# Feed-forward lower products taken one unit at a time instead of the first two as a pair

## The reference

```python
D_FF = 2816
def conv_ffn(h, w_up, w_dw, b_dw, w_down):
    u = dwconv(h @ w_up, w_dw, b_dw)          # 3 taps along the tokens
    a, b = jnp.split(u, 2, axis=-1)
    return (jax.nn.silu(a) * b) @ w_down
...
    h_lat = h_lat + g2 * conv_ffn(b_lat, ffn_w_up[i], ffn_w_dw[i], ffn_b_dw[i], ffn_w_down[i])
    if not last:
        h_ctx = h_ctx + cg2 * conv_ffn(b_ctx, ffn_w_up[i], ffn_w_dw[i], ffn_b_dw[i], ffn_w_down[i])
```

## Time and profile before

| | us |
|---|---|
| median of 3 runs | 2795.96 (2792.84 to 2804.22) |
| profiled execution, its own time | 2798.08 |
| its span | 2796.2 |
| PE busy | 2484.9 (89%) |
| DVE busy | 1188.6 (43%) |
| ACT busy | 856.3 (31%) |
| mean granted TensorE clock | 0.938 of full |

### The profile page before, as it was taken

How to read it: one execution, slowest core, us unless ns; L and a number is a source line. 1 busy time by engine, 2 the same in 40 slices (tenths; PEclk the granted TensorE clock), 3 DMA queues, 4 the chain that set the end, 5 groups by cost and what they waited for, 6 DMA issues and landing times. The chain is left out here.

```text
span 2796.2 us, 35301 instructions
## 1 busy us (share of the span) xinstructions
PE 2484.9 (89%) x14376; PEld 1771.3 (63%) x14376; DVE 1188.6 (43%) x1741; ACT 856.3 (31%) x1305; POOL 29.7 (1%) x57
## 2 busy tenths in 40 slices
PE   5988798999999989899899998888897879999986
PEld 3872477888888776577687876665677653333322
DVE  2688235552355232474563552454333252222323
ACT  4210335331233142384542332455334240100001
POOL 0000000000000001100000000000000000000000
PEclk7998698999999989899899998899899979999998
DMA  5138311121112125101232232210232429999996
GB/s 219 56 98 298 126 47 52 60 75 54 53 60 72 57 99 201 65 2 58 69 102 80 91 106 66 72 54 3 74 99 68 158 85 409 412 410 410 412 415 242
DMA packets 93557, 390.88 MB, mean 140 GB/s; under 512 B 9072, under 2 KB 33904, under 8 KB 65264
## 3 DMA queue, kind: packets, MB, share of 16 engines
q1 hardware_dynamic: 93424, 388.97, 37.4%
HBM read 380.22 MB, written 2.10 MB: 137 GB/s over the span
## 5 line engine op out<-in xcount | busy, mean ns | idle before, releaser
L259 DVE TENSOR_TENSOR WLO<-RAW,WHI 128x1024 fp32r<-128x1024 f32 (+3 forms) x226 | 279.1, 1235 | 807.6 <-ACT WHI L248 807.6
L275 PE MATMUL PS<-XNH,WHI 128*128 128x512 f32 (+1 forms) x1856 | 580.4, 358 | 34.2 <-DVE WLO L259 14.5
L275 PE MATMUL PS<-XNL,WHI 128*128 128x512 f32 (+1 forms) x1856 | 579.9, 357 | 0.0
L275 PE MATMUL PS<-XNH,WLO 128*128 128x512 f32 (+1 forms) x1856 | 575.9, 355 | 0.0
L248 ACT ACTIVATE WHI<-RAW 128x1024 fp32r<-128x1024 f32 (+3 forms) x226 | 241.0, 1068 | 985.4 <-PE PS L275 896.9
L275 PEld LDWEIGHTS PS<-XNH,WHI 128*128 128x128 f32 x1856 | 314.8, 190 | 94.5 <-DVE WLO L259 24.7
L275 PEld LDWEIGHTS PS<-XNH,WLO 128*128 128x128 f32 x1856 | 317.2, 190 | 53.2
L275 PEld LDWEIGHTS PS<-XNL,WHI 128*128 128x128 f32 x1856 | 316.3, 190 | 50.1 <-issue 0.9
L2334 PE MATMUL PS<-RAWM,XS 128*64 128x512 f32 x912 | 216.3, 602 | 19.9 <-DMA RAWM<-experts 19.1
L2334 PEld LDWEIGHTS PS<-RAWM,XS 128*64 128x64 f32 x912 | 59.0, 136 | 144.1 <-issue 77.8
L582 DVE SCALAR_TENSOR_TENSOR C<-V,PRM,C (+1 forms) x120 | 126.0, 1050 | 11.8 <-DVE C L582 9.4
(11 more groups left out here) (309 smaller groups left out, 2975.6 us busy)
## 6 DMA issues: line engine op xcount, KB each, us to landing
RAWM<-experts SPq DMA_DIRECT2D x171, 1024.0 KB, 15.9
ADAW<-ada SPq DMA_DIRECT2D x48, 1024.0 KB, 8.5
RAW<-up SPq DMA_DIRECT2D x88, 512.0 KB, 3.3
RAW<-down SPq DMA_DIRECT2D x32, 704.0 KB, 4.1
X<-experts SPq DMA_DIRECT2D x21, 1024.0 KB, 18.3
RAW<-pw SPq DMA_DIRECT2D x24, 512.0 KB, 3.4
V<-V SPq DMA_DIRECT2D x64, 101.0 KB, 2.6
RAW<-qkv SPq DMA_DIRECT2D x12, 512.0 KB, 3.3
```

Source lines behind the costliest of these rows:

```text
L259: dve.tensor_tensor(prog.WLO[:, at % SPLITS, 0:to.length], prog.RAW[:, at % RAWS, 0:to.length], f32(prog.WHI[:, at % SPLITS, 0:to.length]) ...
L275: last = pe.matmul(prog.PS[:, to, a:b], w, x[:, k, a:b], start=(k == 0 and n == 0), stop=(k == g.k - 1 and n == 2))
```

## The change

A new function `multiply_behind` takes the lower units one at a time, all through `multiply`. Only unit 0 has the waits for the hidden chunks, through the new argument `ready`; the wait for unit 1's weights now stands at the start of unit 1. `conv_ffn` calls it for the lower products of both groups. The number of matmuls is the same.

```diff
--- before.py
+++ after.py
@@ -260,7 +260,7 @@
                       f32(prog.WHI[:, at % SPLITS, 0:to.length]), ALU.subtract).then_inc(prog.weights_lo, 1)
 
 
-def multiply(prog, pe, g, i, s, xh, xl, segments, psum_free, before=0):
+def multiply(prog, pe, g, i, s, xh, xl, segments, psum_free, before=0, ready=None):
 
     slot = (g.base + s) % SPLITS
     pe.wait_ge(prog.weights_lo, g.base + 4 * i + s + 1)
@@ -268,6 +268,8 @@
     to = (before + s) % 4
     last = None
     for k in range(g.k):
+        if ready is not None:
+            ready(k)
         wh = prog.WHI[:, slot, k * P:(k + 1) * P]
         wl = prog.WLO[:, slot, k * P:(k + 1) * P]
         for n, (w, x) in enumerate(((wh, xh), (wh, xl), (wl, xh))):
@@ -296,6 +298,16 @@
                 step(i, s)
     for u in range(4 * max(rounds, 1), g.n):
         step(u // 4, u % 4)
+
+
+def multiply_behind(prog, pe, g, xh, xl, segments, psum_free, ready, before):
+
+
+    multiply(prog, pe, g, 0, 0, xh, xl, segments, psum_free, before, ready)
+    for s in range(1, 4):
+        multiply(prog, pe, g, 0, s, xh, xl, segments, psum_free, before)
+    for u in range(4, g.n):
+        multiply(prog, pe, g, u // 4, u % 4, xh, xl, segments, psum_free, before)
 
 
 def multiply_first(prog, pe, g, xh, xl, segments, psum_free, ready, wait=lambda i, s: None, before=0):
@@ -1007,8 +1019,8 @@
             for grp in range(2):
                 multiply_all(prog, pe, ups[grp], prog.XNH, prog.XNL, lambda u: segments, psum_free,
                              None if grp else chunks_of(pe, norm), before=first(grp, False))
-                multiply_all(prog, pe, downs[grp], HH, HL, lambda u: segments, psum_free,
-                             lambda k: pe.wait_ge(hid_lo[grp], 2 + k + 1), before=first(grp, True))
+                multiply_behind(prog, pe, downs[grp], HH, HL, segments, psum_free,
+                                lambda k: pe.wait_ge(hid_lo[grp], 2 + k + 1), first(grp, True))
 
 
 def collect(prog, g, segments_of, dest_of, loads=(), before=None, load_after=None):
```

## The result

The changed kernel took 2754.41 us (median of 4 runs, 2750.2 to 2769.6) against 2797.26 us; the ratio is 0.9867 with a 95% interval of 0.9841 to 0.9892. Two later comparisons of the same kernel gave 0.9862 (0.9842 to 0.9881) and 0.9898 (0.9879 to 0.9918). All 15 timed executions of it average 2759.4 us, and the 37 of the kernel before in the same and the later comparisons 2794.5: 35.1 us less, where 31.3 was forecast. The three later comparisons ran on different chips, so ratios and differences within one comparison are the safer figures.

A forecast was written before the change was run, and what follows sets the result against it. PE, busy 89% of the span, was taken as the bound, so its idle and half clock cost time. Removing 31.98 us at four places, less 0.7 of new waits, took 2795.96 to 2765 us, range 2757 to 2775.

The forecast's parts named there:

- The gaps: Lower feed-forward units, two places per layer: PE's idle before units 0 and 2 goes, with half clock behind; 31.98 us.
- The wait for chunk 10: Lower unit 0: PE waits 0.34 us for this chunk at each layer 1 place, none in layer 0; costs 0.7 us.
- The dips stay: Rival at the four places: half-clock stretches do not hang on these gaps, only idle goes; 2772.7 us, chance 0.09.
- Chunk 10 binds: Rival in layer 1: both places wait for this chunk and a clock dip follows each; 2767.9 us, chance 0.09.
- Hidden anyway: Rival: a later stage gives the gain back, most likely where DMA is the bound; 2796 us, chance 0.04.
- Slower: Rival in layer 0's second group: unbroken work lowers the clock to 1.2 GHz; 2858 us, chance 0.02.
- The sum: Whole kernel: 31.98 us gained less 0.7 lost gives 31.3 us less, so 2765 us against the median; chance 0.76.
- the pace of units 3 to 7 in the kernel before: Lower units after the change keep this undisturbed pace: 0.353 us a product in layer 0, 0.2267 us a matmul in layer 1.
- dips of other stages: Outside the four places: five half-clock dips falling well, 5 x 1.6 = 8 us, set the range's lower end, 2757.

The follow-up runs named there:

- late_chunk: The changed kernel with unit 0's products of chunk 10 moved behind unit 1's products of chunk 0; 2763.31 us when timed, ratio 0.9892 to the kernel before.
- layer0_only: The kernel before with the change in layer 0 alone, layer 1 keeping the pair; 2781.76 us, ratio 0.9949 to the kernel before.
- lagged: late_chunk with unit 1 running three chunks behind unit 0 in the stages behind a norm; 2760.51 us, ratio 0.9871 to the kernel before.

## Why the prediction was right, and where it fell short

- *The gaps.* Worked out 31.98 us for four places less 0.7. Measured in the profile after, against eight units at the pace of that profile: 0.00, 0.00, 0.32 and 0.32 us are left, so 31.3 us went. The parts fit too: 14.0 + 10.0 us idle and 8.0 half clock before, against 16.6 and 15.3 for the gaps put back one by one.
- *The wait for chunk 10.* 0.34 us at places 3 and 4 and none in layer 0; measured 0.32 each (60.16 - 59.84; 0.45 at the weight load), and late_chunk took it away.
- *The rivals.* "The dips stay" is wrong: the clock was 1.00 through all three stretches of the profile after. "Chunk 10 binds" had the right wait, but no dip followed it: the granted clock of places 3 and 4 was 1.00. The prediction had drawn the dip from the Trainium skill (TensorE: Matmul & The Clock Gate, "A second HAM failure mode: psum-queue depth-cycling"), which tells of short idles between groups of matmuls with which the clock goes up and down; the two idles of 0.3 us here are no case of it. "Hidden anyway" is wrong: the last row of the table of stretches is within 1 us. "Slower" is wrong: the 366 us of unbroken work stood at 1.00.
- *The sum.* It left out a term. The step that failed was "the pace of units 3 to 7 in the kernel before": I took 0.353 us a product pair as a constant of layer 0, and named a pace that left it as a sign that I was wrong. It left it: 0.347 in the profile after, worth 7.0 us of the difference between the profiles from place 1 on, and 3.0 more ahead of it. layer0_only and late_chunk, with the change in layer 0 and the pace at 0.353, show that the change does not force the faster pace. That the first result lies in the range is partly luck: it does by 1.8 us, and the room at that end had been made for dips of other stages and not for the pace.
- *What stays open.* On average over executions the gain was 35.1 us, 3.8 over the forecast; the scatter of the 15 and 37 executions (6.7 and 4.1 us) puts some 3.6 us on that difference at 95%, so the surplus stands at the edge of what chance makes. The three comparisons taken singly gave 40.7, 37.7 and 29.7 us by averages. But of the eight profiles with the change in layer 0, five had the faster pace between places 1 and 2, and of the five with a gap left there one had. That is too few to say whether a restart behind a gap favours the slower pace. If the shares held (5 of 8 against 1 of 5), an estimate from them is 0.4 of 3.5 to 7 us, so that 1.5 to 3 us more would belong to the change.

## What to carry to other kernels

When two units share each inner chunk as it comes, they also start and end together: the first one's start waits for both units' weights, and the buffers of both come free at once. Compare the time until the last chunk is there with one unit's work on the chunks ahead of it. If the work covers it, take the units in turn: here it did in layer 0 (8.5 us until the chunk, 10.6 of work) and just failed to in layer 1 (6.9 and 6.8), where a wait of 0.3 us was left. A unit's pace from its undisturbed neighbours times the number of units, taken from the measured stretch, gives idle and clock loss in one subtraction, and was right to a few tenths. The gaps of two or three us cost a third as much again through the clock behind them (24.0 and 8.0 us). A profile taken to see one edit should be compared stretch by stretch: with late_chunk and lagged most of the difference lay in a stage that the edit does not touch.

## What the runs showed of the hardware that was not expected

- At the same granted clock of 1.00 a pair of matmuls of 512 and 256 columns started every 0.3533 or every 0.3467 us, 1.9% apart. In 13 profiles the pace of the stretch that starts near 455 us was the slower one in six and the faster in seven; three programs (before, late_chunk, lagged) were seen at both; in no profile did it change inside the unbroken stretches, and in three of the five profiles with gaps left in layer 0 it differed between the upper units ahead of place 1 and those behind it. The matmuls of 512 columns in layer 1 kept 0.2267 us in all of them. What sets it was not found; over layer 0's feed-forward it is worth 10 us, so one profile's difference of that size may be no effect of an edit.
- The same kernel's executions spread by 22 us (2749.9 to 2771.5 for the changed one), more than the profile's places do (303.36 to 303.42 us in three profiles). The ratios of its three comparisons differed by 0.0036.
- A dip of the clock follows some idles of PE and not others. In the profile before, the granted clock in the 3.4 us behind the eight gaps of the four places (two at each, in order) was 1.00, 0.51, 0.62, 1.00, 0.58, 0.63, 1.00 and 0.65: five dips, 8.0 us together, and an idle of 3.3 us stood ahead of the 1.00 at place 4. In the last expert, at one and the same wait, the three profiles with an idle of 2.08 us had half clock behind it and the ten with 0.55 to 1.73 us had 1.00; there the idle that was at most 1.5 us longer made the stretch some 5 us longer.
